# Weight pieces of a decoder trunk: six raw buffers and three split pairs, split two pieces ahead, for four of each and three ahead

## What is computed

```
for i in range(2):
    h = rmsnorm(x, norm_g[i, 0])
    o_mix, q_mem = mixer(h, w_in[i])                 # one wide input projection
    o_mem = memory_attention(q_mem, rmsnorm(mem, norm_g[i, 4]), w_mem_kv[i])
    x = x + rmsnorm(concat([o_mix, o_mem]) @ w_o[i], norm_g[i, 1])
    h = rmsnorm(x, norm_g[i, 2])
    f = (silu(causal_conv3(h @ w_gate[i]) + b) * (h @ w_up[i])) @ w_down[i]
    x = x + rmsnorm(f, norm_g[i, 3])
```

## Time and profile before

| | us |
|---|---|
| runs: median of 3 (lowest, highest) | 2399.86 (2399.73, 2402.75) |
| profiled execution, own time | 2401.63 |
| its span, first to last instruction | 2399.8 |
| PE busy | 2301.8 |
| PEld busy | 1901.4 |
| DVE busy | 1302.1 |
| ACT busy | 1182.3 |
| DMA share of the raw pieces' queue (16 engines) | 56.2% |
| granted TensorE clock, mean over the span | 0.983 |

### The profile page before, as it was taken

The page is one execution under the profiler, slowest core; times in us unless marked ns, Lnnn a source line. Parts: engine busy times, 40 slices in busy tenths (PEclk is TensorE's granted clock), DMA queues, the critical chain, the costliest instruction groups (busy, mean ns, idle before and its releaser), DMA issues.

```text
span 2399.8 us, 26702 instructions
## 1 busy us (share of the span) xinstructions
PE 2301.8 (96%) x10618; PEld 1901.4 (79%) x10618; DVE 1302.1 (54%) x1575; ACT 1182.3 (49%) x1613; POOL 109.5 (5%) x88
## 2 busy tenths in 40 slices
PE   7999999999999999999879999999999999999996
PEld 5887778788888888888657887787888888888885
DVE  6554445555555555444354666655555555554443
ACT  5545565555555555444354544445555545554442
POOL 3000000200000000000031000002000000000002
PEclk9999999999999999999989999999999999999998
DMA  6545555466656566666445752354665665566663
GB/s 243 173 150 162 152 165 177 148 191 185 185 185 186 186 187 203 192 193 193 146 157 154 253 168 88 106 154 144 193 186 183 186 190 178 191 204 194 193 193 119
DMA packets 115868, 422.36 MB, mean 176 GB/s; under 512 B 13216, under 2 KB 13216, under 8 KB 114976
## 3 DMA queue, kind: packets, MB, share of 16 engines
q1 hardware_dynamic: 115136, 417.98, 56.2%
q10 hardware_dynamic: 432, 2.15, 0.2%
q0 software_dynamic: 176, 0.53, 0.1%
HBM read 418.51 MB, written 2.10 MB: 175 GB/s over the span
## 4 chain that ended last, share of the span: by engine, by line
PE 92%; DVE 3%; POOL 2%; ACT 1%; issue 1%; DMA 1%; SPq 0%; POOLq 0%; DVEq 0%; ACTq 0%
PE bank L475 88%; PE bank L582 2%; POOL y L1188 1%; DVE lo L956 1%; DMA raw<-in_mem 1%; PE bank L563 0%; POOL x L1189 0%; DVE amem L962 0%; DVE x L1033 0%; POOL blkf L1231 0%; DMA raw<-in_down 0%; DVE sp L1058 0%; ACT ab L845 0%; ACT ab L844 0%; ACT hi L743 0%
## 5 line engine op out<-in xcount | busy, mean ns | idle before, releaser
L956 DVE TENSOR_TENSOR lo<-raw,hi 128x1024 fp32r<-128x1024 f32 (+1 forms) x777 | 953.0, 1233 | 915.0 <-ACT hi L743 913.1
L475 PE MATMUL bank<-hi,h 128*128 128x512 f32 x3904 | 1243.5, 394 | 7.0 <-DVE lo L956 4.5
L743 ACT ACTIVATE hi<-raw 128x1024 fp32r<-128x1024 f32 (+1 forms) x777 | 819.8, 1058 | 796.1 <-PE bank L475 752.9
L475 PEld LDWEIGHTS bank<-hi,h 128*128 128x128 f32 x3904 | 736.3, 189 | 159.9 <-DVE lo L956 5.0
L475 PE MATMUL bank<-lo,h 128*128 128x512 f32 x1952 | 762.9, 391 | 0.0
L475 PE MATMUL bank<-hi,mid 128*128 128x512 f32 x1408 | 435.9, 390 | 8.9 <-DVE lo L956 8.9
L475 PEld LDWEIGHTS bank<-lo,h 128*128 128x128 f32 x1952 | 368.5, 189 | 72.7
L475 PEld LDWEIGHTS bank<-hi,mid 128*128 128x128 f32 x1408 | 265.4, 189 | 64.3 <-DVE lo L956 9.3
L475 PE MATMUL bank<-lo,mid 128*128 128x512 f32 x704 | 274.8, 390 | 0.0
L475 PE MATMUL bank<-hi,o 128*128 128x512 f32 x512 | 164.7, 395 | 1.1 <-DVE o L1048 1.1
L475 PEld LDWEIGHTS bank<-lo,mid 128*128 128x128 f32 x704 | 132.7, 189 | 27.7
(11 more groups left out here) (185 smaller groups left out, 1126.1 us busy)
## 6 DMA issues: line engine op xcount, KB each, us to landing
raw<-in_gate SPq DMA_DIRECT2D x176, 512.0 KB, 4.3
raw<-in_up SPq DMA_DIRECT2D x176, 512.0 KB, 3.6
raw<-in_down SPq DMA_DIRECT2D x176, 512.0 KB, 4.3
raw<-in_in SPq DMA_DIRECT2D x136, 512.0 KB, 3.7
raw<-in_out SPq DMA_DIRECT2D x64, 512.0 KB, 3.7
raw<-in_mem SPq DMA_DIRECT2D x32, 512.0 KB, 4.5
raw<-in_cmp SPq DMA_DIRECT2D x16, 512.0 KB, 4.4
memT<-in_memT SPq DMA_DIRECT2D x8, 512.0 KB, 6.1
```

The costliest lines, as they stand in the source:

```text
L475: return mm(out, lhsT, rhs, start=first, stop=last, skip_group_check=True)
L743: act(hi[k][:, 0:w], raw[k][:, 0:w], ACT.Copy).then_inc(hi_done, 1)
L956: tt(lo[k][:, 0:w], raw[k][:, 0:w], hi[k][:, 0:w].bitcast(F32), ALU.subtract).then_inc(lo_done, 1)
```

## The change

There are six buffers for raw pieces and three each for `hi` and `lo`: 12 of 4 KB per partition as before. `load(n)` waits for `lo` of piece n-6. `round_piece(n)` waits until TensorE has finished piece n-3. Rounding and split of piece n+2, where it was n+3, open tick n on ACT and DVE. The loops still start at tick -3, so the steps of ticks -3 to -1 stay where they were; piece 0 is rounded at tick -2. The order of SP's loads and steps is not touched.

```diff
-RING = 4
-LEAD = 3
+RAW = 6
+RING = 3
+LEAD = 2
...
-        raw = [sb(f"raw{k}", [P, 2 * W]) for k in range(RING)]
+        raw = [sb(f"raw{k}", [P, 2 * W]) for k in range(RAW)]
         hi = [sb(f"hi{k}", [P, 2 * W], F32R) for k in range(RING)]
         lo = [sb(f"lo{k}", [P, 2 * W], F32R) for k in range(RING)]
...
-        landed = [sem(f"landed{k}") for k in range(RING)]
+        landed = [sem(f"landed{k}") for k in range(RAW)]
...
             def load(n):
                 c, p = PLAN.pieces[n]
-                k = n % RING
-                if n >= RING:
-                    sp_.wait_ge(lo_done, n - RING + 1)
+                k = n % RAW
+                if n >= RAW:
+                    sp_.wait_ge(lo_done, n - RAW + 1)
                 sp_.dma_start(raw[k][:, 0:size(c)], kv_piece(c, p)).then_inc(landed[k], 16)
...
             def round_piece(n):
                 c, _ = PLAN.pieces[n]
-                k, w = n % RING, size(c)
-                act_.wait_ge(landed[k], 16 * (n // RING + 1))
+                k, r, w = n % RING, n % RAW, size(c)
+                act_.wait_ge(landed[r], 16 * (n // RAW + 1))
                 if n >= RING:
                     act_.wait_ge(piece_done, n - RING + 1)
-                act(hi[k][:, 0:w], raw[k][:, 0:w], ACT.Copy).then_inc(hi_done, 1)
+                act(hi[k][:, 0:w], raw[r][:, 0:w], ACT.Copy).then_inc(hi_done, 1)
...
-            for n in range(-LEAD, TICKS):
-                if n + LEAD < TICKS:
+            for n in range(-3, TICKS):
+                if 0 <= n + LEAD < TICKS:
                     round_piece(n + LEAD)
...
             def split_piece(n):
                 c, _ = PLAN.pieces[n]
-                k, w = n % RING, size(c)
+                k, r, w = n % RING, n % RAW, size(c)
                 dve.wait_ge(hi_done, n + 1)
-                tt(lo[k][:, 0:w], raw[k][:, 0:w], hi[k][:, 0:w].bitcast(F32), ALU.subtract).then_inc(lo_done, 1)
+                tt(lo[k][:, 0:w], raw[r][:, 0:w], hi[k][:, 0:w].bitcast(F32), ALU.subtract).then_inc(lo_done, 1)
...
-            for n in range(-LEAD, TICKS):
-                if n + LEAD < TICKS:
+            for n in range(-3, TICKS):
+                if 0 <= n + LEAD < TICKS:
                     split_piece(n + LEAD)
```

## The result

The changed kernel runs in 2418.11 us (median of 4, 2416.78 to 2422.93), the kernel before on the same chip in 2399.95: a ratio of 1.0076 with the interval 1.0063 to 1.0088. It is slower, by 15 to 21 us. The profiled execution of the changed kernel took 2416.78 us, 15.15 more than that of before; its span is 2415.0.

What follows compares the result with a forecast made beforehand. TensorE's matmul stream, busy 96% of the span, was taken as the bound. Terms 10.3 + 3.4 + 0.4 + 0.1 + 0.5 = 14.7 us, against 2399.86, gave 2414.5 us; range 2405 to 2423.

Steps and rivals of the forecast that it cites:

- the split of n takes the place of the split of n+1: All pieces: each split ends where the next piece's ends now, unless a landing set it; margin negative for 39 of 777.
- FFN pairs: 22 FFN pairs: the split of u,5, behind convB, comes too late for TensorE; 0.47 us each, +10.3 us.
- Windows: Layer 1, splits held until windows are made: waits at 424 and 428, +3.4 us; small lack at piece 458, +0.4.
- Between the layers: Post and angles between the layers: earlier chain to x against a later split of 397; two opposing effects, +0.1 us.
- "paid in full" rival: No order gain between the layers, 8 us added at 397, windows 6.8: 2426 us; chance 0.13.
- order gain: Between the layers: post's first square directly behind the rounding of 393, making the chain to x 1.65 us earlier.
- The start: First pieces: piece 0 rounded behind the first amem pair, x loads issued ahead of raw 2's landing; +0.5 us.
- the same work under the same POOL work ends at about the same time: Start, before piece 2: reordered amem and lo operations on DVE finish about as before while POOL squares; within the +0.5 us.
- Loads: All loads: 5.4 us more room each, buying nothing, since SP's program order delays the loads of 383 and 393.
- The sign that ACT's waits for cmp pieces vanish: Profile after, on ACT: waits for landings of cmp and up pieces vanish without gain; no size given.
- "faster" rival: Pieces 383 and 393: six raw buffers carry TensorE past SP's two waits, -19.5 us, giving 2395; chance 0.04.
- The clock: FFN: rival that each of 22 short waits brings a low-clock piece, 57 us in all, 2472 us; chance 0.03.

Runs made afterwards that it cites:

- experiment 8: Changed kernel with ACT's part of angles 12 ticks later, POOL's part where it was: 2408.49 us, ratio 1.0032.
- old_sp_late: Kernel before (four and four, three ahead) with SP's reload and small loads four ticks later: 2377.76 us, ratio 0.9904.
- old_moves: Kernel before with SP's reload and small loads, ACT's angles and the windows' ACT and DVE parts moved later: 2368.85 us, ratio 0.9869.
- start_old: Changed kernel with the old order at the start only: pieces 0, 1, 2 rounded and split at ticks -3, -2, -1: 2417.28 us.
- ring3_lead3: Changed kernel with the split three pieces ahead, keeping three split pairs and six raw buffers: 2428.82 us, ratio 1.0116.
- windows_late: Changed kernel with the ACT and DVE parts of windows two ticks later, POOL's part where it was: 2414.18 us, ratio 1.0056.
- lead2_ring4: Kernel before (four raw buffers, four split pairs) with only the split two pieces ahead instead of three: 2419.92 us, ratio 1.0082.
- sp_late: Changed kernel with SP's reload of the memory tokens and three small loads four ticks later: 2399.45 us, ratio 0.9998.
- experiments 2 and 5: Four raw buffers instead of six, in the changed kernel (2417.84 us) and in the changed kernel with SP's reload and small loads four ticks later (2399.51 us).

## Why the prediction was right

The time (2418.11 for 2414.5) and its sign came from the rule that the split of n takes the place of the split of n+1. Its terms, in the order of the prediction:

- **FFN pairs, +10.3 predicted.** All 22 pairs show the wait at u,5: it starts 0.28 us later in the first pair and 0.35 in the others, 5.5 + 5.6 = 11.1 us in all, 0.50 per pair. 0.35 is the lack and the 0.06 us; the rest, 0.15 us, is the restart, where I took 0.11. Moving convB alone brought 10.9 us back: shown. In all seven other traces with the split two ahead and convB where it was, the pairs cost 5.4 to 5.5 us per layer.
- **Windows, +3.4 and +0.4.** By the starts of 423 and 431 it is 3.7 us, and 0.3 more by piece 460. Piece 424 waits 4.07 us (about 4 was forecast), 428 2.46 us (2.4). PE and DVE after, against the earlier trace rows:

```profile
1324.32 0.47 PE L476 MATMUL bank<-hi,blk 128*60 128x256 f32 x1 [4.07 <-DVE lo L957]
...
1335.95 0.33 PE L476 MATMUL bank<-hi,blk 128*60 128x256 f32 x1 [2.46 <-DVE lo L957]
1338.17 0.80 PE L476 MATMUL bank<-hi,h 128*128 128x512 f32 x1 [1.07 <-DVE lo L957]
1342.53 0.28 PE L476 MATMUL bank<-hi,blk 128*60 128x256 f32 x1
```

```profile
1323.05 3.49 DVE L957 TENSOR_TENSOR lo<-raw,hi 128x1024 fp32r<-128x1024 f32 x3
1327.47 1.23 DVE L957 TENSOR_TENSOR lo<-raw,hi 128x1024 fp32r<-128x1024 f32 x1 [0.93 <-ACT hi L744]
...
1334.15 6.24 DVE L957 TENSOR_TENSOR lo<-raw,hi 128x1024 fp32r<-128x1024 f32 x4
```

  The sum held by luck, since two steps in it were off and cancel. Piece 425 was to end 1.2 us late; it ends where it did before (0.0 against piece 423), since it ran in 3.55 us instead of 5.28, at a granted clock of 0.77 instead of 0.50. So 429 starts only 2.2 us late and not 3.4. But then it took 1342.53 - 1338.17 = 4.36 us instead of 2.85, at a granted clock of 0.63 instead of 1.00, and I had not counted that.
- **Between the layers, +0.1.** Measured -0.4 (5.6 to 5.3). Both effects are there. ACT after, against the earlier trace rows:

```profile
1208.26 1.06 ACT L744 ACTIVATE hi<-raw 128x1024 fp32r<-128x1024 f32 x1 [9.07 <-DMA raw<-in_mem]
1209.22 0.58 ACT L820 ACTIVATE mf<-bank 128x512 f32<-128x512 f32 x1
...
1234.31 0.31 ACT L879 ACTIVATE sinf<-red 128x128 f32<-128x128 f32 x1 [8.68 <-POOL red L1205]
```

  Post's first square follows the landing's rounding by 0.96 us instead of 2.71; the wait for x fell from 11.43 to 9.16 us; and the wait for the split of 397 came, 7.92 us. The "paid in full" rival failed here: the order gain that it left out came (2.6 us by the starts of 392 and 394), and of the 8.2 us that the wait at 397 adds, 6.0 are back by 399, chiefly because before TensorE stood 6.05 us for h there. Without the angles' wait this place is a gain, as experiment 8 shows.
- **The start, +0.5.** This is the term that was mis-sized. In the profiled execution of after it is 0.2 us, but that execution is the exception. Piece 2 starts there at 23.8 us, and at 25.6 to 26.1 in the eight other traces with the new order at the start; with the old order (before, old_sp_late, old_moves, start_old, ring3_lead3) it starts at 23.0 to 23.6. Piece 4 starts at 31.0 (after) and 31.3 to 33.9 us (windows_late the earliest, lead2_ring4 the latest), with the old order at 30.2 to 31.7: 1.8 us more in the mean. The step that failed is "the same work under the same POOL work ends at about the same time". DVE's first pair of amem operations that meets POOL's squares, in the trace of after, then of sp_late:

```profile
10.54 2.51 DVE L963 SCALAR_TENSOR_TENSOR amem<-memT,gains,amem 128x256 fp32r<-128x256 f32 x2
```

```profile
10.76 4.62 DVE L963 SCALAR_TENSOR_TENSOR amem<-memT,gains,amem 128x256 fp32r<-128x256 f32 x2
```

  In after POOL's second square begins at 10.67, behind DVE's first operation of the pair, which takes 0.48 us; in sp_late it begins at 10.49, ahead of it, and both operations are slow. And the split of piece 1 now stands behind this pair and takes 2.91 to 3.40 us; before, it began ahead of that square and took 1.23. The earlier x did hold raw 2 back, as the Trainium skill's rule on interleaving ("DMA: Bandwidth & Descriptors", Issuing engines are not separate DMA queues) says: the rounding that waits for it starts at 16.6 instead of 14.4 us, and at 15.8 to 16.8 in all nine traces with the new order, with four raw buffers as with six, against 13.8 to 14.4 with the old. The trace agrees. But this never reached TensorE. ACT, DVE and PE, after:

```profile
16.56 1.06 ACT L744 ACTIVATE hi<-raw 128x1024 fp32r<-128x1024 f32 x1 [4.65 <-DMA raw<-in_mem]
```

```profile
16.30 4.62 DVE L963 SCALAR_TENSOR_TENSOR amem<-memT,gains,amem 128x256 fp32r<-128x256 f32 x2
20.84 2.91 DVE L957 TENSOR_TENSOR lo<-raw,hi 128x1024 fp32r<-128x1024 f32 x1
```

```profile
23.80 0.77 PE L476 MATMUL bank<-hi,amem 128*128 128x512 f32 x1 [4.36 <-DVE lo L957]
```

  Piece 2's rounding was done at 17.6, but DVE, which doesn't stand still from 8.5 to 27 us, reached its split only at 20.84. So up to piece 2 it is DVE's order against POOL that costs the time. From piece 2 to piece 4 the traces with the new order take 5.6 to 8.3 us and those with the old 7.1 to 8.3; what sets that stays open, and so does how much of the runs' median the start explains.
- **Loads.** Nothing was gained by them, as forecast; experiments 2 and 5 show it with and without SP's two waits. The sign that ACT's waits for cmp pieces vanish came true, but that for up pieces can't be held against anything: the list of before has no such wait. The "faster" rival's places were right, and its price near (18.7 us on the changed kernel, for 19.5; on the one before 23.5); what it needed was another order on SP and not the buffers.
- **The clock.** It did not fall in the FFN. The granted clock of the two FFN stretches, after:

```profile
448.00:960.00 512.00, 509.97 (x2335) 420.35 (x2334) 283.04 (x322) 271.01 (x341) 2.60 (x2) 1.00 0.59 184
...
1687.00:2154.00 467.00, 464.91 (x2118) 382.98 (x2117) 256.73 (x288) 240.53 (x287) 0.00 (x0) 1.00 0.60 184
```

  So what the Trainium skill ("TensorE: Matmul & The Clock Gate", A second HAM failure mode) tells of frequent short idle gaps did not come true here: with one start 0.35 us late in every 46 us the clock stays at 2.4 GHz.

## What to carry to other kernels

A split or a load that is prepared "k pieces ahead" stands at a fixed place among its engine's other steps. To judge a smaller k, take the times at which that engine finishes item n+1 today and hold them against the consumer's start on n; every place where this is negative costs its lack plus a restart, unless TensorE would stand idle soon after anyway (the 8.1 us that piece 397 lacked cost nothing by piece 399), and a fourth split pair doesn't change it. More transfer buffers can gain only where a transfer is late; here the late ones were late because the issuing queue stood in a wait ahead of them, and moving that wait by four ticks gained 18.7 us, with four buffers as with six.

## What was not expected of the hardware

- After 2.46 us of idleness, 8 short matmuls and another wait of 1.07 us TensorE began the next piece at the low clock (granted clock 0.63 over the piece, 0.80 us for the first matmul, 4.36 us for the piece), while a single wait of 1.31 us before was followed by a piece of 2.85 us at a granted clock of 1.00.
- DVE operations against POOL operations are not slowed by a steady factor: the same pair took 0.87, 2.51 or 4.62 us, depending on whether POOL's operation had begun ahead of it.
